# An mLSTM scan with two pairs of banks for its own products, a later scatter in the expert stage, and activation tables loaded ahead

## The reference

```
# experts: the two best of eight per token
for e in range(N_EXPERTS):
    out = out + gates[..., e:e + 1] * swiglu(x, w_gate[e], w_up[e], w_down[e])
# mLSTM, one chunk of 128 tokens, per head and direction
qk  = (q @ k.T) * w                                   # w: decay weights, 0 above the diagonal
num = a * (C @ q) + qk @ v                            # past products, own products
den = a * (n . q) + sum(qk)                           # past sums, own sums
h   = num / max(|den|, exp(-m))
# output of the layer: o * (h_forward + h_backward), then a layer norm per head
# around each sublayer of the second block
x = x + g * rms_norm(y);   hx = rms_norm(x) * (1 + scale) + shift
```

## Time and profile before

| | |
|---|---|
| median of 3 runs | 3096.33 us (3094.85 to 3098.14) |
| the profiled execution | 3098.8 us, of it 3097.0 us from the first to the last instruction |
| mean granted TensorE clock | 0.955 |
| PE busy | 2894.9 us, 93% |
| VectorE busy | 1898.5 us, 61% |
| ScalarE busy | 1448.2 us, 47% |
| DMA, expert stage (800 to 1800 us) | share 0.90 to 0.95, 335 to 357 GB/s |

### The profile page before, as it was taken

The page is one execution under the profiler, slowest core; times in us unless marked ns, Lnnn a source line. Parts: engine busy times, 40 slices in busy tenths (PEclk is TensorE's granted clock), DMA queues, the critical chain, the costliest instruction groups (busy, mean ns, idle before and its releaser), DMA issues. The chain is left out here.

```text
span 3097.0 us, 39311 instructions
## 1 busy us (share of the span) xinstructions
PE 2894.9 (93%) x15789; PEld 2281.6 (74%) x15789; DVE 1898.5 (61%) x2304; ACT 1448.2 (47%) x1833; POOL 13.5 (0%) x13
## 2 busy tenths in 40 slices
PE   8999899999999999999999989999789999899798
PEld 5799799797667676676766767558667777757796
DVE  4655455546788888888888832334554544445675
ACT  4211254444676666666666733223243333343554
POOL 0000000000000000000000000000000000000000
PEclk9999799998999999999999999999689999999899
DMA  5300365645998998989989972310022222200352
GB/s 183 130 1 1 150 233 189 259 150 212 365 351 334 357 344 335 358 334 351 344 338 362 355 303 87 90 47 4 6 71 95 96 83 95 82 35 28 123 188 97
DMA packets 94032, 585.88 MB, mean 189 GB/s; under 512 B 20400, under 2 KB 21504, under 8 KB 24480
## 3 DMA queue, kind: packets, MB, share of 16 engines
q1 hardware_dynamic: 92704, 581.52, 50.6%
q10 hardware_dynamic: 1152, 1.88, 0.2%
HBM read 582.31 MB, written 1.05 MB: 188 GB/s over the span
## 5 line engine op out<-in xcount | busy, mean ns | idle before, releaser
L2291 DVE TENSOR_TENSOR s_w_low<-weight_ring,s_w_high 128x2048 fp32r<-128x2048 f32 x336 | 759.7, 2289 | 129.3 <-ACT s_w_high L2231 125.5
L2231 ACT ACTIVATE s_w_high<-weight_ring 128x2048 fp32r<-128x2048 f32 x336 | 630.2, 1909 | 132.3 <-PE bank L2213 105.8
L262 DVE TENSOR_TENSOR s_w_low<-weight_ring,s_w_high 128x1024 fp32r<-128x1024 f32 x254 | 309.1, 1222 | 224.9 <-ACT s_w_high L244 224.0
L244 ACT ACTIVATE s_w_high<-weight_ring 128x1024 fp32r<-128x1024 f32 x254 | 266.8, 1053 | 307.9 <-PE bank L642 275.5
L2213 PE MATMUL bank<-s_w_high,s_x_low 128*96 128x512 f32 x896 | 355.9, 397 | 7.2 <-issue 7.2
L642 PE MATMUL bank<-s_x_high,s_w_low 128*128 128x256 f32 (+1 forms) x1056 | 340.4, 322 | 23.0 <-DVE s_x_low L723 14.8
L2213 PE MATMUL bank<-s_w_high,s_x_high 128*96 128x512 f32 x896 | 356.3, 398 | 0.0
L2213 PE MATMUL bank<-s_w_low,s_x_high 128*96 128x512 f32 x896 | 353.9, 395 | 0.0
L642 PE MATMUL bank<-s_x_low,s_w_high 128*128 128x256 f32 (+1 forms) x1056 | 338.9, 321 | 0.0
L642 PE MATMUL bank<-s_x_high,s_w_high 128*128 128x256 f32 (+1 forms) x1056 | 338.6, 321 | 0.0
L642 PEld LDWEIGHTS bank<-s_x_high,s_w_low 128*128 128x128 f32 x1056 | 203.6, 193 | 41.0 <-DVE s_w_low L262 21.4
(11 more groups left out here) (510 smaller groups left out, 4602.6 us busy)
## 6 DMA issues: line engine op xcount, KB each, us to landing
weight_ring<-moe_w SPq DMA_DIRECT2D x336, 1024.0 KB, 7.0
weight_ring<-ada_w SPq DMA_DIRECT2D x48, 1024.0 KB, 7.2
weight_ring<-ffn_up SPq DMA_DIRECT2D x44, 1024.0 KB, 4.8
weight_ring<-ffn_w_in SPq DMA_DIRECT2D x22, 1024.0 KB, 4.8
weight_ring<-ffn_down SPq DMA_DIRECT2D x22, 1024.0 KB, 4.8
weight_ring<-ffn_w_down SPq DMA_DIRECT2D x11, 1024.0 KB, 4.8
weight_ring<-w_rkv_cols SPq DMA_DIRECT2D x8, 1024.0 KB, 16.2
weight_ring<-moba_qk SPq DMA_DIRECT2D x8, 1024.0 KB, 12.5
```

The lines of the kernel that those rows point to most:

```text
L244: K.nc.scalar.activation(self.hi[:, b, :], self.source(c, i), ACT.Copy).then_inc(*self.high.up())
L262: K.nc.vector.tensor_tensor(self.lo[:, b, :], self.source(c, i), self.hi[:, b, :], ALU.subtract)\
L2231: nc.scalar.activation(halves(whi, kind, n, i), raw(kind, n, i), ACT.Copy).then_inc(S["high"].h, 1)
L2291: V.tensor_tensor(halves(wlo, kind, n, i), raw(kind, n, i), halves(whi, kind, n, i), ALU.subtract)\
```

## The change

Three groups of edits. In the expert stage the second half of the scatter, and of the adds, goes one step and two turns later respectively than the first half. In the scan the own products of odd tiles go to banks 0 and 1, all one-column sums follow the products and wait for the reciprocal of the tile before, `mix` is cut into `divide` and `mix` with the norm of the tile before (and the weighing of a later tile) between them, and the turning over of the first two tiles is moved between the last tile's sums and its past products. In the tails a one-element Sqrt into a junk buffer (now 8 columns wide) is issued on ScalarE ahead of the first wait, and `passage` takes the first tile's root before the second tile's squares, with the second tile's `total` behind the first tile's scaled result.

```
+def table(K, act, fn):
+    n = 1 + K.warmed % 7
+    K.warmed += 1
+    K.nc.scalar.activation(K.junk[:, n:n + 1], K.ones[:, 0:1], fn)
...
# post_norm, ahead of the copy of the gains; adaln, ahead of square(2)
+            table(K, act, ACT.Sqrt)
...
# routed_experts, PE
-                if e and p in (1, 2):
-                    scatter(e - 1, p - 1)
+                if e and p in (1, 3):
+                    scatter(e - 1, p // 2)
# routed_experts, VectorE
-            if 0 < e < NE and p in (1 + DEEP, 2 + DEEP):
-                add(e - 1, p - 1 - DEEP)
+            if 0 < e < NE and p in (1 + DEEP, 3 + DEEP):
+                add(e - 1, (p - DEEP) // 2)
...
# passage, ScalarE
-        for tt in range(min(2, tts)):
-            square(tt)
+        table(K, act, ACT.Sqrt)
+        square(0)
         for s in range(tts + (2 if nxt else 0)):
             if s < tts:
                 act.wait_ge(*summed.at(s + 1))
                 nc.scalar.activation(root[:, s:s + 1], root[:, s:s + 1], ACT.Sqrt).then_inc(*rooted.up())
+            if s == 0:
+                square(1)
# passage, VectorE
-            if s + 1 < tts:
+            if 0 < s < tts - 1:
                 total(s + 1)
...
                 K.v(dve, last)
+            if s == 0:
+                total(1)
...
# mlstm, PE
+    own_bank = lambda i, d: (0 if i % 2 else 3) + d
+    flip_bank = (2, 3, 4, 0)
...
-                pe.wait_ge(*(mixed.at(i) if i else grown.at(3)))
+                pe.wait_ge(*(grown.at(3) if i == 0 else weights.at(8) if i == 1 else mixed.at(i - 1)))
                 for d in range(2):
                     for h in range(4):
-                        nc.tensor.matmul(K.ps[3 + d][:, head(h)], W[:, i, d, h, :], vrow[:, tt, head(h)],
+                        nc.tensor.matmul(K.ps[own_bank(i, d)][:, head(h)], W[:, i, d, h, :], vrow[:, tt, head(h)],
                                          start=True, stop=True)
-                        nc.tensor.matmul(K.ps[7][:, o + 4 * d + h:o + 4 * d + h + 1], W[:, i, d, h, :],
-                                         K.ones[:, 0:1], start=True, stop=True)
+                if i:
+                    pe.wait_ge(*scaled.at(i))
+                for n in range(8):
+                    nc.tensor.matmul(K.ps[7][:, o + n:o + n + 1], W[:, i, n // 4, n % 4, :], K.ones[:, 0:1],
+                                     start=True, stop=True)
+                if i == 3:
+                    flip(0)
+                    pe.wait_ge(*mixed.at(3))
+                    flip(1)
                 if i:
                     pe.wait_ge(*read.at(i))
...
-            for i in range(4):
-                pe.wait_ge(*normed.at(i + 1))
...
+            flip(2)
+            flip(3)
# mlstm, VectorE (divide is the old mix up to the wait for ScalarE, mix the rest)
-            for i in range(4):
+            divide(0)
+            weigh(2)
+            mix(0)
+            for i in range(1, 4):
+                divide(i)
+                norm(i - 1)
+                if i == 1:
+                    weigh(3)
                 mix(i)
-                if i + 2 < 4:
-                    weigh(i + 2)
-                norm(i)
+            norm(3)
```

More of the change, by code:

```diff
@@ L95, in __init__ @@
         self.ones = sb("ones", [P, P])
-        self.junk = sb("junk", [P, 1])
+        self.junk = sb("junk", [P, 8])
         self.wide = sb("condition_wide", [P, KT, 32])
@@ L101, in __init__ @@
         self.paired = 0
+        self.warmed = 0
         self.nphase, self.uniq = 0, 0
@@ L1953, in _ @@
                 for s in (K.dense_hid, K.dense_added, K.dense_turned):
-                    K.v(dve, V.memset(K.junk[:, :], 0.0), s)
+                    K.v(dve, V.memset(K.junk[:, 0:1], 0.0), s)
             @block.scalar
@@ L2345, in vector @@
         for n in range(2):
-            V.memset(K.junk[:, :], 0.0).then_inc(K.used.h, 1)
+            V.memset(K.junk[:, 0:1], 0.0).then_inc(K.used.h, 1)
             dve.wait_ge(K.used.h, u0 + n + 1)
@@ L3110, in _, with flip @@
             row(3)
+            def flip(i):
+                pe.wait_ge(*normed.at(i + 1))
+                for h in range(4):
+                    last = nc.tensor.transpose(K.ps[flip_bank[i]][:, head(h)], hrow[:, order[i], head(h)], K.ident[:, :])
+                last.then_inc(*flipped.up())
             for i in range(4):
@@ L3114, in _ @@
                     score(i + 2)
-            for i in range(4):
-                pe.wait_ge(*normed.at(i + 1))
-                for h in range(4):
-                    last = nc.tensor.transpose(K.ps[i][:, head(h)], hrow[:, order[i], head(h)], K.ident[:, :])
-                last.then_inc(*flipped.up())
+            flip(2)
+            flip(3)
         @block.vector
@@ L3137, in state, with divide @@
                 K.v(dve, last, grown)
-            def mix(i):
+            def divide(i):
                 tt, o = order[i], 32 + 16 * i
@@ L3160, in mix @@
                 K.v(dve, last)
+            def mix(i):
+                tt, ds = order[i], [d for d in range(2) if step[i][d]]
                 dve.wait_ge(*mixed.at(i + 1))
@@ L3236, in _ @@
                         to = hrow[:, order[i], head(h)] if d == 0 else other[:, i % 2, head(h)]
-                        last = nc.scalar.activation(to, K.ps[3 + d][:, head(h)], ACT.Copy, scale=den[:, d, h:h + 1])
+                        last = nc.scalar.activation(to, K.ps[own_bank(i, d)][:, head(h)], ACT.Copy, scale=den[:, d, h:h + 1])
                 last.then_inc(*mixed.up())
@@ L3242, in _ @@
                 act.wait_ge(*flipped.at(i + 1))
-                nc.scalar.activation(yT[:, 4:8, cols(order[i])], K.ps[i][:, :].rearrange("p (h t) -> p h t", h=4), ACT.Copy)\
+                nc.scalar.activation(yT[:, 4:8, cols(order[i])],
+                                     K.ps[flip_bank[i]][:, :].rearrange("p (h t) -> p h t", h=4), ACT.Copy)\
                     .then_inc(*placed.up())
@@ L3391, in _ @@
             rotate(ckv[:, 0:TT, P:160], lambda f, ax: rope[:, :, f, ax, :], TT)
-            K.v(dve, V.memset(K.junk[:, :], 0.0), spun)
+            K.v(dve, V.memset(K.junk[:, 0:1], 0.0), spun)
             for tt in range(TT):
@@ L3406, in _ @@
                        lambda f, ax: bc(rope[:, tt, f, ax, :].unsqueeze(1), [P, H, 8]), H)
-                K.v(dve, V.memset(K.junk[:, :], 0.0), turned)
+                K.v(dve, V.memset(K.junk[:, 0:1], 0.0), turned)
             for n in range(8):
```

## The result

In the first comparison the changed kernel took 3051.02 us (median of 4 runs, 3043.3 to 3055.55) and the kernel before 3095.59 (4 runs); the ratio is 0.9853, 95% interval [0.983, 0.9875]. A second comparison gave 0.9856 [0.983, 0.9883]. The interval of the ratio reaches from 3043.7 to 3057.6 us, so on which side of 3051 the time came out is chance; that the sum was short by 8.7 us is not.

A forecast was written before the change was run, and what follows sets the result against it. PE was taken as the bound, busy 93% of the span, so only its stops or lower clock could be won. 16.6 + 12.9 + 7.3 = 36.8 us off the median 3096.3 gave 3059.5 us, range 3051 to 3069.

The forecast's parts named there:

- 16.6 us taken: Expert stage: moving the second scatter one step later removes seven PE stops of 2.37 us each, 16.6 us.
- the rival of a new wait for weights: Expert stage: gives nothing because a wait for weights (DMA or low parts) replaces the stop; 3076.1 us, chance 0.08.
- 12.9 us taken: Scan: new order ends the last norm at 2210.2 instead of 2223.05, the middle clock case, 12.9 us less.
- Here I let the clock fall: Scan: PE idles 2.6 us before the third tile's past products, and the clock falls as after 2.8 us before.
- past(2) and past(3): Scan: past products of the third and last tiles, forecast to end at 2185.0 and 2198.7.
- own(3) with sums: Scan: the last tile's own products and row sums, forecast to run from 2185.0 to 2191.8.
- The upper bound of 19.9: Scan: if the clock stays high throughout, the end is 2203.2, 19.9 us less.
- the rival of a high clock: Scan: the clock stays high, fewer stops, total 3052.5 us; chance 0.15.
- I take the high clock until PE next stands still: Scan: own products and sums fill the stretch where PE stopped 2.8 us, so the clock stays high until the next stop.
- the rival of the one-column sums: Scan: clock low from the second tile on, since one-column sums give PE little to do; 3062.6 us, chance 0.15.
- 7.3 us taken: Tails: square root table ahead and new order save 0.7, 1.9, 1.9 and 2.8 us in four tails, 7.3 us.
- post_norm and adaln, 0 taken: Table loads there gain nothing: PE runs modulation products beside them, or VectorE is busy with statistics until after the root.

The follow-up runs named there:

- before_filled: Kernel before, with nine unused 128-column products ahead of each of TensorE's three scan waits for the scaling; 3090.7 us, ratio 0.9971.
- only_scan: Kernel before with only the scan's part of the change; 3083.86 us, ratio 0.9942.
- only_tails: Kernel before with only the tails' part, square root tables ahead and new order; 3094.38 us, ratio 0.9978.
- tables_alone: Kernel before with only the square root's tables loaded ahead, old order of the tails; 3097.97 us, ratio 0.9984.
- order_alone: Kernel before with only the new order of the tails, no table loaded ahead; 3097.58 us, ratio 0.9995.
- one_pair: Changed kernel with own products of all tiles back in banks 3 and 4, waiting for the previous tile's scaling; 3062.48 us, ratio 0.9883.
- gain_filled: gain_columns plus five unused 128-column products in TensorE's wait before the third tile's past products; 3045.86 us, ratio 0.9836.
- gain_columns: Changed kernel with the norm's gain applied by ScalarE as columns and the divisor's magnitude in one VectorE operation; 3045.94 us, ratio 0.9837.

## Why the prediction was right about PE's stops and wrong about the clock

- **Expert stage, 16.6 us taken, 19.7 to 20.4 measured.** The stops went as worked out: 2.37 us each, nothing queued behind them, and the rival of a new wait for weights did not come (PE busy 124.70 of 124.70 us at a DMA share of 0.93). The term left out what a stop costs behind it: two of seven periods had 1.56 us more from the lower level, 3.1 us, and 16.6 + 3.1 = 19.7. One step had stood for all seven. The other profiles bear this out: with two such periods the stage takes 1002.0 us (before, before_filled), with three 1002.8 to 1003.3 us (only_scan, only_tails, tables_alone, order_alone), and in the eight profiles without the stops no period has it and the stage takes 981.5 to 982.3 us.
- **Scan, 12.9 us taken, 17.5 (two profiles) and 19.4 (one) measured. This is the step that failed:** "Here I let the clock fall", and after it I let it stay low to the end, at 5.3 us for past(2) and past(3), 6.8 for own(3) with sums, and 1.8 for the two turns. The stop came where it was forecast (2.0, 2.3 and 0.65 us against 2.6), and the clock did fall, to 0.50, at the longer ones (within their first us), but some 8 us behind their end, in which PE had no stop, it was at 1.00 again. Then past(3) and the turns took half, and VectorE, not PE, set the end. I had carried over the course of before, where the clock stayed down for 44 us; there each low stretch held another stop for the scaling. one_pair brings these stops and the 0.50 back (54.1 us); before_filled shortens them in the old order and wins 9.8 us; gain_filled fills one, and the fall with its 2.38 us is gone. The upper bound of 19.9 held, the rival of a high clock (0.15) was nearly the case of the first profile. The premise "I take the high clock until PE next stands still" failed too: the clock fell for 3.4 us at 2140 and again at 2147 with PE busy throughout. So the rival of the one-column sums was not refuted in its mechanism; what did not come is a clock that stays low.
- **What carries the scan's gain.** Without the second pair of banks the scan is 14.2 to 16.1 us longer, without VectorE's division 5.4 to 7.3, without the early turns 1.4 to 3.3 (against 39.95 and 38.06). These are prices of undoing one from the end, not shares.
- **Tails, 7.3 us taken, 7.8 and 8.7 measured.** 0.57, 2.58, 2.82 and 2.75 us by tail against 0.7, 1.9, 1.9 and 2.8. The chain of the last one was right to 0.1 us. In the third, PE's work behind its stop for the diagonal took 5.33 instead of 6.20 us, at a mean clock of 0.71 instead of 0.60. In the second, 0.8 us come and go with the clock: 27.36 us in only_tails and gain_filled, 26.6 in the other profiles with both parts. That a shorter stop brings the higher clock is not shown.
- **post_norm and adaln, 0 taken.** adaln lies between the last start of the experts' product line and the next phase's first product (L355 of before). That stretch scatters from 76.4 to 79.4 us over kernels with and without the load (gain_filled with it 77.4, order_alone without 79.3), so a gain or loss below 3 us stays open. The post_norm calls lie in the stretch that scatters by 15 us, and the runs can't tell what they gave.
- **Sum.** With what was measured, 19.7 + 17.5 + 7.8 = 45.0 at the low ends, and 20.4 + 19.4 + 8.7 = 48.5 at the high ones. The range's low end counted the upper bounds of the scan (19.9) and tails (8) but held the experts' 16.6 as their best case: 44.5, where 45.0 to 45.5 came. Of the 8.7 us that the sum was short, 4.6 to 6.5 are the scan's, 3.1 to 3.8 the experts'.

## What to carry to other kernels

Price a stop of TensorE by what it does to the products behind it as well: look at the granted clock in the 10 us after each of its kind, not after one. When an edit takes out one of several stops, ask of each low stretch whether it holds another stop that keeps it low; if the edit removes that one too, the clock comes back and the engine next in line sets the pace. Look also for falls with no stop ahead of them, which an edit that only removes waits won't take away. A wait that can't be removed may be filled with products that are not used.

## What the runs showed of the hardware that was not expected

- The place of the expert stage's start differs by 15 us between executions, 774.4 to 789.8 us in 14 profiles; kernels identical up to there in the work that they do (before and only_scan) had 781.7 and 789.1. A difference of up to 0.5% between two single profiles can be this alone. The granted clock of the stretch 300 to 350 us was 0.70 in before and 0.78 after; whether such stretches explain all of it was not tested.
- The same scan of the changed kernel ran in two courses, 38.06 and 39.95 us, with PE's stop at 0.65 or 2.31 us. Both have a first fall of 3.4 us near the start; the next came at 2147.0 and lasted 3.4 us in the one, and at 2157.9, for 10 us, in the other.
- A stop as short as 0.88 us (gain_columns) stood ahead of a fall to 0.50; one of 1.52 us (after, at 2163.40) and one of 1.40 us (gain_filled, at 2158.23) did not. And the clock fell to 0.50 with no stop at all (after, at 2140 and 2147, PE busy 18.4 of the 18.4 us from 2132 to 2150.4). What tells them apart is open.
- Nine unused products of 128 columns took 2.17 us at the full clock, and at three places they made the scan 9.8 us shorter.
